# Two FFN norms without the row scaling: the reciprocal roots are multiplied into the up product by GpSimd

## The reference, cut to what matters

```python
def rms_norm(x, g):
    y = x * lax.rsqrt(jnp.mean(x * x, axis=-1, keepdims=True) + RMS_EPS)
    return y * g

def conv_ffn(x, w_up, conv_w, conv_b, w_down):
    u = causal_dwconv(x @ w_up, conv_w, conv_b)      # 3 taps along the tokens
    g, v = u[..., :D_FF], u[..., D_FF:]              # D_FF = 3072
    return (jax.nn.gelu(g, approximate=True) * v) @ w_down

    # in each layer of the first model
    h = rms_norm(x, norm_ffn_pre[layer])
    h = conv_ffn(h, ffn_w_up[layer], ffn_conv_w[layer], ffn_conv_b[layer], ffn_w_down[layer])
    x = x + rms_norm(h, norm_ffn_post[layer])
```

## Time and profile before

| | |
|---|---|
| median of 3 runs | 1335.41 us (1330.8 to 1339.57) |
| the profiled execution | 1335.4 us span, which is its own time |
| PE / weight load / DVE / ACT / POOL busy | 1264.9 / 1080.7 / 913.2 / 695.0 / 77.0 us |
| up stage, layer 0 | 308.48 to 441.60 us |
| up stage, layer 1 | 611.94 to 745.00 us |
| PE's pause ahead of layer 0's up stage | from 299.11 us |
| PE's pause ahead of layer 1's up stage | from 603.70 us |

### The profile page before, as it was taken

The page is one execution under the profiler, slowest core; times in us unless marked ns, Lnnn a source line. Parts: engine busy times, 40 slices in busy tenths (PEclk is TensorE's granted clock), DMA queues, the critical chain, the costliest instruction groups (busy, mean ns, idle before and its releaser), DMA issues.

```text
span 1335.4 us, 19244 instructions
## 1 busy us (share of the span) xinstructions
PE 1264.9 (95%) x7760; PEld 1080.7 (81%) x7760; DVE 913.2 (68%) x1429; ACT 695.0 (52%) x1132; POOL 77.0 (6%) x126
## 2 busy tenths in 40 slices
PE   7999999999999999999999999999979889899997
PEld 5899988877888887987888876786758876788885
DVE  4464553447888857687888876755796886766665
ACT  5454544446666645766666755334332444455553
POOL 1000000001000001001000001022011301000000
PEclk9999999999999999999999999999989899899999
DMA  9844335556555557257555557212533006555551
GB/s 336 327 172 145 127 126 190 189 186 241 192 189 192 186 200 265 93 190 291 189 190 189 189 189 266 72 64 103 165 124 101 2 1 212 200 189 191 191 200 48
DMA packets 31718, 230.74 MB, mean 173 GB/s; under 512 B 11000, under 2 KB 14704, under 8 KB 18704
## 3 DMA queue, kind: packets, MB, share of 16 engines
q1 hardware_dynamic: 25568, 218.14, 45.3%
q10 hardware_dynamic: 5056, 7.73, 1.6%
q0 software_dynamic: 1008, 3.67, 0.7%
HBM read 225.82 MB, written 3.71 MB: 172 GB/s over the span
## 4 chain that ended last, share of the span: by engine, by line
PE 78%; DVE 12%; ACT 6%; issue 2%; DMA 1%; POOL 1%; SPq 0%; DVEq 0%; POOLq 0%; ACTq 0%
PE ps L436 18%; PE ps L620 16%; PE ps L499 10%; PE ps L440 9%; PE ps L208 8%; PE ps L488 5%; PE ps L587 4%; DVE parts L344 3%; PE ps L559 3%; PE ps L531 2%; ACT parts L340 2%; DMA ring<-in_W 1%; DVE arena L1655 1%; DVE row L1908 1%; DVE arena L1906 1%
## 5 line engine op out<-in xcount | busy, mean ns | idle before, releaser
L344 DVE TENSOR_TENSOR parts<-ring,parts 128x1024 fp32r<-128x1024 f32 x354 | 431.4, 1224 | 278.5 <-ACT parts L340 201.0
L340 ACT ACTIVATE parts<-ring 128x1024 fp32r<-128x1024 f32 x354 | 372.7, 1057 | 296.6 <-PE ps L440 102.6
L436 PE MATMUL ps<-hall,parts 128*128 128x512 f32 x1120 | 395.1, 398 | 5.5 <-DVE hall L293 3.7
L440 PE MATMUL ps<-hall,parts 128*128 128x256 f32 x1120 | 313.8, 280 | 0.0
L620 PE MATMUL ps<-parts 128*128 128x512 f32 x1128 | 262.0, 391 | 8.6 <-DVE parts L375 8.3
L436 PEld LDWEIGHTS ps<-hall,parts 128*128 128x128 f32 x1120 | 211.1, 188 | 58.4 <-issue 3.3
L620 PEld LDWEIGHTS ps<-parts 128*128 128x128 f32 x1128 | 210.0, 188 | 57.9 <-DVE parts L375 12.6
L440 PEld LDWEIGHTS ps<-hall,parts 128*128 128x128 f32 x1120 | 212.3, 190 | 0.0
L499 PE MATMUL ps<-hall,parts 128*128 128x256 f32 x1152 | 140.7, 284 | 0.0
L499 PEld LDWEIGHTS ps<-hall,parts 128*128 128x128 f32 x1152 | 139.0, 192 | 0.6 <-DVE parts L344 0.5
L208 PE MATMUL ps<-arena 128*128 128x128 f32 (+4 forms) x934 | 111.7, 285 | 16.4 <-DMA arena<-in_onehot 6.5
(11 more groups left out here) (213 smaller groups left out, 1066.0 us busy)
## 6 DMA issues: line engine op xcount, KB each, us to landing
ring<-in_W SPq DMA_DIRECT2D x100, 2048.0 KB, 8.3
arena<-distance_tables SPq DMA_DIRECT2D x8, 384.0 KB, 8.0
gains<-in_gains POOLq DMA_DIRECT2D x5, 512.0 KB, 8.1
ring<-in_W SPq DMA_DIRECT2D x4, 512.0 KB, 9.1
arena<-in_gate_w ACTq DMA_DIRECT2D x1, 2048.0 KB, 10.6
matrices<-arena ACTq DMA_DIRECT2D x8, 256.0 KB, 2.3
x<-in_x SPq DMA_DIRECT2D x2, 512.0 KB, 5.3
gates<-in_ada_gate_b POOLq DMA_DIRECT2D x2, 512.0 KB, 6.3
```

What stands on the lines that cost most here:

```text
L340: return nc.scalar.activation(unit_weights(n, 0, weights), weights, ACT.Copy)
L344: return nc.vector.tensor_tensor(unit_weights(n, 1, weights), weights, unit_weights(n, 0, weights), ALU.subtract)
L436: last = nc.tensor.matmul(ps[:, b, :].rearrange("p (a b) -> p a b", a=2), w[:, 0, :], hparts[:, :, k, :], start=k == 0, stop=False)
L440: last = nc.tensor.matmul(ps[:, b, 0:S], w[:, 1, :], hparts[:, 0, k, :], start=False, stop=k == KT - 1)
```

## The change

For the two FFN norms of the first model (`rows_scaled=False`, `roots_index`):

- DVE no longer scales x, and PE transposes x itself, each half row as soon as x is ready. ACT squares x for this norm after the columns have been taken out, so that the roots come during the first chunk.
- `spread`: PE multiplies the column of 128 roots, broadcast, with the identity, once for each t, so that each partition holds the roots of all tokens; this stands ahead of the fourth unit of the first chunk. ACT copies the result to `roots` (`spread_out`) ahead of its first L413.
- `rooted`: for each chunk POOL multiplies `up_sum` by `roots` in place, in two instructions of 128 x 512 (units 0 and 1, then 2 and 3). ACT's taps wait for the instruction that has their units; DVE's list for a chunk is unchanged.
- `low_beside`: POOL makes the low part of the second unit of each up stage (128 x 1024) ahead of the norm's roots; DVE leaves it out.
- PE's order in the pause (`beside_unscaled_norm`): transposes of t = 0, first `ada`, transposes of t = 1, other `ada`s, all turns, and the same wait for the last `ada_out`. In the pause ACT and DVE have their work in another order: one high part between the two squares of t = 1, DVE's first `ada_out` behind the fourth column, in layer 1 the second one behind the eighth column.
- On POOL the load of the next gain (`load_gain`, which waits until it has landed) now stands behind `low_beside` and ahead of `rooted`.
- Some semaphores are merged, and `wait`s for low parts go through `low_ready`.

```diff
+            def spread(self, pe):
+                pe.wait_ge(S_("norm_rstd"), TT * self.index + TT)
+                for t in range(TT):
+                    c = slice(self.col + t, self.col + t + 1)
+                    last = mm(ps[:, self.banks[3], t * P:(t + 1) * P], smallp[:, c].to_broadcast([P, P]), ident, True, True)
+                last.then_inc(S_("roots_spread"), 1)
+
+            def spread_out(self, act, count):
+                act.wait_ge(S_("roots_spread"), count)
+                nc.scalar.activation(roots[:, :], ps[:, self.banks[3], 0:S], ACT.Copy).then_inc(S_("roots"), 1)
...
+                            if self.rows_scaled:
+                                pe.wait_ge(S_("norm_scaled"), ...)
+                            else:
+                                self.ready(pe, t, k // 4)
...
+        def low_beside(pool, n):
+            weights = UNITS[n][1]
+            pool.wait_ge(S_("high_parts"), n + 1)
+            nc.gpsimd.tensor_tensor(unit_weights(n, 1, weights), weights, unit_weights(n, 0, weights), ALU.subtract).then_inc(S_("low_aside"), 1)
...
+            def rooted(self, pool):
+                pool.wait_ge(S_("roots"), self.roots_index + 1)
+                by_unit = roots[:, :].unsqueeze(1).to_broadcast([P, 2, S])
+                for j in range(len(self.chunks)):
+                    self.sum_ready(pool, j)
+                    for pair in range(2):
+                        two = up_sum[j % 2][:, 2 * pair:2 * pair + 2, :]
+                        nc.gpsimd.tensor_tensor(two, two, by_unit, ALU.mult).then_inc(S_("up_rooted"), 1)
...
@@ SplitUp.tensor
+                        if self.roots_index is not None:
+                            if j == 0 and n == 3:
+                                norm.spread(pe)
+                            if j == 1 and n == 3:
+                                pe.wait_ge(S_("roots"), self.roots_index + 1)
...
@@ POOL
             r_mix0.pool(pool)
+            low_beside(pool, up_ffn0.first + 1)
             n_ffn0.pool(pool)
             load_gain(2)
+            up_ffn0.rooted(pool)
...
@@ gated_ffn on ACT
-                    up.sum_ready(act, j)
                     for n in range(4):
+                        up.rooted_ready(act, j, n)
...
@@ ACT, layer 0 (layer 1 alike, with ada_rows(5), ada_rows(6))
             r_mix0.square(act, 0)
+            r_mix0.square(act, 1, [0])
+            high_parts(act, up_ffn0.first + 1)
+            r_mix0.square(act, 1, [1])
             high_parts(act, up_ffn0.first + 2)
-            r_mix0.square(act, 1)
+            ada_rows(2)
+            n_ffn0.evacuate(act, 0, range(0, 4))
+            high_parts(act, up_ffn0.first + 3)
+            n_ffn0.evacuate(act, 0, range(4, 8))
             n_ffn0.square(act, 0)
-            ada_rows(2)
             n_ffn0.square(act, 1)
-            high_parts(act, up_ffn0.first + 3)
-            n_ffn0.evacuate(act, 0)
             high_parts(act, up_ffn0.upto(0))
+            n_ffn0.spread_out(act, 1)
...
@@ DVE, layer 0
             r_mix0.add(dve, 0)
-            low_parts(dve, up_ffn0.first + 1)
             r_mix0.gained(dve, 1)
             r_mix0.add(dve, 1)
-            n_ffn0.scale(dve, 0)
-            n_ffn0.scale(dve, 1)
-            low_parts(dve, up_ffn0.first + 2)
+            low_parts(dve, up_ffn0.first + 1)
+            n_ffn0.evacuate(dve, 1, range(0, 4))
             ada_out(2)
-            n_ffn0.evacuate(dve, 1)
+            n_ffn0.evacuate(dve, 1, range(4, 8))
...
@@ DVE, layer 1
-            n_ffn1.scale(dve, 0)
+            low_parts(dve, up_ffn1.first + 1)
+            n_ffn1.evacuate(dve, 1, range(0, 4))
             ada_out(5)
-            n_ffn1.scale(dve, 1)
-            low_parts(dve, up_ffn1.first + 1)
+            n_ffn1.evacuate(dve, 1, range(4, 8))
             ada_out(6)
-            n_ffn1.evacuate(dve, 1)
...
@@ PE
+            def beside_unscaled_norm(first, end, residual, norm):
+                norm.tensor(pe, [0])
+                ada(first)
+                norm.tensor(pe, [1])
+                for i in range(first + 1, end):
+                    ada(i)
+                for i in range(first, end):
+                    ada_turn(i)
+                pe.wait_ge(S_("ada_out"), end)
+
-            beside_norm(2, 3, r_mix0, n_ffn0)
+            beside_unscaled_norm(2, 3, r_mix0, n_ffn0)
...
-            beside_norm(5, 7, r_mix1, n_ffn1)
+            beside_unscaled_norm(5, 7, r_mix1, n_ffn1)
```

More of the change, by code:

```diff
@@ L204, in build_program @@
         lT = region(8192, KT, S)
+        roots = region(31232, S)
         lgw = region(20992, 2, 4, 2, S)
@@ L228, in build_program, with __init__ @@
         class Norm:
-            def __init__(self, index, col, src, scaled, dst, gain, shift, ready, banks=(4, 5, 6, 7), into=hparts, shifted_before=0, paired=False):
-                self.paired = paired
+            def __init__(self, index, col, src, scaled, dst, gain, shift, ready, banks=(4, 5, 6, 7), into=hparts, shifted_before=0, paired=False,
+                         rows_scaled=True, unscaled_before=0):
+                self.paired, self.rows_scaled, self.unscaled_before = paired, rows_scaled, unscaled_before
                 self.into, self.shifted_before = into, shifted_before
@@ L262, in vector_scale, with tensor @@
                     self.scale(dve, t)
[L264 to L265 removed]
+            def spread(self, pe):
[7 more added lines that the diff above has]
+                nc.scalar.activation(roots[:, :], ps[:, self.banks[3], 0:S], ACT.Copy).then_inc(S_("roots"), 1)
+            def tensor(self, pe, halves=range(TT)):
+                for t in halves:
                     for k in range(KT):
                         if k % 4 == 0:
[L268 to L269 removed]
+                            if self.rows_scaled:
+                                pe.wait_ge(S_("norm_scaled"), 2 * (TT * (self.index - self.unscaled_before) + t) + k // 4 + 1)
+                            else:
+                                self.ready(pe, t, k // 4)
+                        rows = self.scaled if self.rows_scaled else self.src
+                        last = nc.tensor.transpose(self.turned(k)[:, t * P:(t + 1) * P], rows[:, t, k * P:(k + 1) * P], ident)
                         if t == TT - 1 and (k % 2 if self.paired else k // 2 % 2):
@@ L329, in build_program, with low_ready @@
         ahead = []
+        aside = []
+        def low_ready(eng, n):
+            if n in aside:
+                eng.wait_ge(S_("low_aside"), aside.index(n) + 1)
+            else:
+                eng.wait_ge(S_("low_parts"), n + 1 - sum(m < n for m in aside))
         def high_weights(act, n):
@@ L628, in unit @@
             def unit(self, pe, kk):
-                pe.wait_ge(S_("low_parts"), self.first + kk + 1)
+                low_ready(pe, self.first + kk)
                 self.products(kk, 0, kk % 4 == 3)
@@ L668, in step, with square @@
                 return 2 * (TT * self.index + t) + half + 1
-            def square(self, act, t):
-                for half in range(2):
+            def square(self, act, t, halves=range(2)):
+                for half in halves:
                     self.y_ready(act, t, half)
@@ L727, in build_program @@
         p_mix0 = SplitProjection(0, [("wo", i, 0) for i in range(2)], oT, KT, lambda e, kk: e.wait_ge(S_("oT"), kk + 1))
-        up_ffn0 = SplitUp([("up", 0, j) for j in range(12)], 0, 0)
+        up_ffn0 = SplitUp([("up", 0, j) for j in range(12)], 0, 0, 0)
         p_ffn0 = SplitProjection(1, [("down", 0, i) for i in range(6)], aT, FT, lambda e, kk: e.wait_ge(S_("aT"), kk // 2 + 1))
@@ L731, in build_program @@
         p_mix1 = SplitProjection(2, [("lout", i, 0) for i in range(2)], lT, KT, lambda e, kk: e.wait_ge(S_("lT"), kk // 2 + 1))
-        up_ffn1 = SplitUp([("up", 1, j) for j in range(12)], 12, 0)
+        up_ffn1 = SplitUp([("up", 1, j) for j in range(12)], 12, 0, 1)
         p_ffn1 = SplitProjection(3, [("down", 1, i) for i in range(6)], aT, FT, lambda e, kk: e.wait_ge(S_("aT"), 12 + kk // 2 + 1))
@@ L1004, in _ @@
             r_mix1.pool(pool)
+            low_beside(pool, up_ffn1.first + 1)
             n_ffn1.pool(pool)
             load_gain(4)
+            up_ffn1.rooted(pool)
             n_ctx.pool(pool)
@@ L1264, in _ @@
             r_mix1.square(act, 0)
-            r_mix1.square(act, 1)
+            r_mix1.square(act, 1, [0])
+            high_parts(act, up_ffn1.first + 1)
+            r_mix1.square(act, 1, [1])
+            high_parts(act, up_ffn1.first + 2)
+            ada_rows(5)
+            n_ffn1.evacuate(act, 0, range(0, 4))
+            ada_rows(6)
+            high_parts(act, up_ffn1.first + 3)
+            n_ffn1.evacuate(act, 0, range(4, 8))
+            act.dma_start(ctxx[:, :, :], A["ctx"].rearrange("(t p) d -> p t d", p=P)).then_inc(S_("ctx_in"), 16)
             n_ffn1.square(act, 0)
-            ada_rows(5)
             n_ffn1.square(act, 1)
-            for i in range(6, 7):
-                ada_rows(i)
```

(5 more changed lines are left out.)

88 lines of the change are left out of this document (45 added, 43 removed).

## The result

| | before | after |
|---|---|---|
| median | 1337.49 us (4 runs, 1330.8 to 1341.14) | 1397.33 us (4 runs, 1395.07 to 1400.7) |
| ratio after / before | | 1.0442, 95% interval 1.0417 to 1.0467 |
| the profiled execution's span | 1335.4 us | 1396.7 us |

The change makes the kernel 4.4% slower. The direction was forecast, the size was not: 1379 was predicted, 1390 was the upper end of the range. (The profiled execution after took 1398.5 us, 1.8 more than its span; the prediction took span and time for one.

The account below looks back on a forecast made before the run. PE was taken as the bound, with DVE's loop just under it and overtaking it once POOL multiplies: 1335.4 + 2 x 22.1 (loops, tails) + 2 x 0.9 (spreading) - 2.5 + 0.5 (pauses) = 1379 us, range 1352 to 1390.

Parts of the forecast that it names:

- What bounds the kernel, and the loop: Up stages: PE sets 11.09 us a chunk, DVE's loop 0.24 under it; POOL's multiplies lengthen the loop to 12.99.
- The turn: Up stages: POOL's multiply and DVE's low part L344 take turns, one turn lost a chunk, +0.98 us.
- The loops, in us: Up stages, first to last sum: eleven loops a layer, each 1.90 us longer, 20.9 us a layer.
- of which a cushion takes 0.7. That leaves 1.2: Behind each layer's last sum: the next low part comes 1.90 us late, 0.7 absorbed, 1.2 lost.
- x is ready at 606.97 as before: Layer 1's pause: x no later than before; the whole pause loses 0.5 us, bounds -1.0 and +1.5.
- the second `ada_out`, and PE starts at some 614.0: Layer 1's pause: two `ada` pieces in line with the columns, first unit over at 616.8; 0.5 us lost.
- The pause of layer 0: Start of layer 0's up stage: removed square, roots and scaling gain 2.0 to 3.1 us, 2.5 taken.
- Spreading the roots: First chunk of each layer: two PE matmuls 0.4 us and ACT's copy 0.5, together 0.9 a layer.
- (a): Up stages: no turns lost between POOL and DVE, 1358 us; chance 0.22.
- (b): Up stages: PE's clock also falls behind each chunk's pause, 19 us more, 1398; chance 0.09.
- (c): Faster: the loop's cost vanishes in slack or idle time, pauses' gains remain, 1328 us; chance 0.04.
- (d): Near nothing: multiplies faster than their rows and the pauses' gains full, 1340 us; chance 0.05.

Follow-up runs that it names:

- e3: The changed kernel with DVE's low part behind the sum moved behind the other taps, so nothing of DVE runs beside POOL's multiplies; 1466.95 us, ratio 1.0986.
- e1: The changed kernel without POOL's multiplies, the taps waiting for the sum again (roots left out of the result); 1349.92 us, ratio 1.0090.
- e2: The kernel before with POOL's 48 multiplies added, by ones, in the place the change gives them; 1388.51 us, ratio 1.0390.
- e5: The changed kernel with layer 1's first high part moved behind the last square of the mixer's rows; 1391.11 us in one run.
- e6: The changed kernel with the second unit's low part moved from POOL back to DVE; 1396.76 us in one run.
- e7: The changed kernel with the edits of e4, e5 and e6 together, POOL still multiplying; 1363.94 us, ratio 1.0207.
- e11: The changed kernel without multiplies, second unit's low part on DVE, layer 1's ada pieces ahead of the transposes of t = 1; 1338.62 us, ratio 1.0004.
- e4: The changed kernel with DVE's other taps and ACT's gelu of each chunk done one chunk later; 1371.85 us, ratio 1.0261.
- e10: The changed kernel with POOL multiplying the sum by constant one, reading one input, roots left out; 1393.35 us in one run.
- e9: The changed kernel with POOL writing ones into the sum instead of multiplying it; 1348.87 us in one run.

## Why the prediction was wrong, point by point

- **What bounds the kernel, and the loop.** Right: DVE's loop stood a little under PE's pace, and POOL's step made it the bound; the taps' wait names POOL. The period was forecast at 12.99 and is 13.29, by two terms. From the sum to the other taps 4.28 was forecast and 4.77 measured, because the multiply was taken at 1.02 us, from a row where one operand is broadcast along the inner dimension, and costs 1.27 in this place (e3). The rest of the loop was taken at 8.71 and is 8.52, because 0.19 us of it was a wait. So the slack was 0.24 + 0.19 = 0.43 us, not 0.24. The turn was right to the hundredth, 0.98 (e3).
- **The loops, in us.** Measured 44.5 more for both layers, forecast 41.8; that this is so near is luck in part. The prediction took 11.09 us a chunk for both layers, for layer 1 from a window that ends 4.3 us ahead of the stage's end, and PE's pace there was 11.30. The loops were forecast at 142.9 us each (11 x 12.99) and are 146.3 and 146.0. In layer 1 a period too short by 0.3 and a pace before too short by 0.2 cancel: 20.9 forecast, 21.1 measured.
- **The tail, "of which a cushion takes 0.7. That leaves 1.2".** Wrong in this profile: 4.4 and 4.2 us. The cushion was read in the middle of a stage; where the down product begins, each split has 256 more columns to do, and PE then stood 3.14 us for one low part and lost more at a granted clock of 0.50 behind it. e1, without the multiplies, has the tails of before. How the 4.4 us divide between the late part and the clock I did not separate, and they are not firm: e2, e5 and e6, with the same multiplies, have 1.8 us in layer 0 (61.35 to 61.40), near the forecast, and 2.5 to 5.5 in layer 1. In the changed kernel's profile the two tails are short by 6.2 us in all.
- **The pause of layer 1, "x is ready at 606.97 as before".** This is the step that failed most: the stretch is short by 9.0 us. Counted from the first square, x was ready at 7.31 us before and is at 13.49 now, 6.2 later. I priced what the moved high part delays by its own 1.06 us, in layer 0 alone, and did not ask what it waits for itself. It waits for a transfer, 4.56 us, and with the square ahead of it x is ready at 7.23 again (e5). POOL's low part beside the adds, 2.1 of the 6.2 us, was weighed for layer 0 only. A second step failed here, "the second `ada_out`, and PE starts at some 614.0": with x in time, the stretch is still 3.6 us longer (e7), where the pieces in line and the spreading had been priced at 1.4. The second turn (1.02 us on PE) waits for the first `ada_out` and was left out, and the clock falls to 0.50 in the first unit, which the sum had at nothing.
- **The pause of layer 0.** -1.6 forecast with the spreading, +0.5 measured. The low part taking its turn ahead of DVE's second add was the bad bound there, and it is what happens (e6: 2.3 us). I had priced it at 1.2, and taken half of that. Without it the forecast is near: -1.8 (e6).
- **Spreading the roots.** Nothing in the rows speaks against 0.9 a layer. It was not tried alone.
- **The rivals.** (a), no turns lost, is out. (b), the clock, is not what the loop shows: a whole round, with a wait of 1.94 us, has a granted clock of 1.00, and the loop of 13.3 us is accounted for without it. It acts in the pauses and the tail, and in e3's loops, where the wait is 3.51 us (0.90). The prediction's sum had no term for it in the pauses. (c) and (d) are out, and e11 shows that (c)'s 9 us of pauses were not there in this order either: they stand at 0.4.
- **The range** ended at 1390 because its upper end had bounds for the turn and the pauses as they were read, and nothing for the places that were costed at one value: the multiply, the tails, the wait for the transfer.

In all: forecast +44.0, measured +61.3 in the profile; 9.0 + 6.2 + 2.1 for the pauses and tails, 2.7 for the loops, less 2.7 in stretches that the change doesn't touch.

## What to carry to other kernels

When work is moved to an idle engine, look for the loop it is put into: here a second engine had 1.16 us of idle time a chunk, and yet only some 0.4 us of slack, as the idle time was a wait inside that loop. When a list is reordered, ask of each moved instruction what it waits for itself, a transfer above all, before asking what waits for it. And before building, test the ceiling by leaving the costly part out: e11 shows that with these pauses the idea gives nothing even for free.

## What the runs showed of the hardware

- GpSimd's elementwise instructions with two inputs and VectorE's with two SBUF inputs take turns here, whole instructions at a time, and either side can be the loser: L370 2.17 in place of 1.22 us, eight other taps 4.40 in place of 3.37 (e4), two adds 3.55 in place of 1.41 behind one POOL instruction of 2.34. With one input on GpSimd's side the loss is 0.2 us of L370 (e10), and with none it is nothing (e9).
- GpSimd's multiply of 128 x 512 takes 1.27 us here and 1.02 where one operand is broadcast along the inner dimension; whether that is the reason is not tested. The multiply by a constant, with one input, takes longer: 1.49 and 1.59 (e10). Writing ones takes 1.00 for two.
- PE's pace with all engines keeping up is 11.09 us a chunk in some stretches and about 11.3 in others, at a granted clock of 1.00 in both: 122.84 us of loops in layer 0 and 124.87 in layer 1 before, 124.99 and 124.88 in e11. What sets this stays open; it is worth 2 us a layer, so differences of that size between two profiles are not to be put down to an edit.
